# Three small reorderings on the matrix engine of a two-layer hybrid decoder: chunk states signalled one by one, value products half a gate later, spare products in other gaps

## What is computed

```
mod = silu(c) @ w_ada[l] + b_ada[l]                   # conditioning: six vectors of 1024
h   = rms_norm(x) * (1 + sc1) + sh1
gq, gk, gv, ga, gr, sq, sk, sv, mix_a, mix_b = split(h @ w_in[l])
# gated linear attention, 4 heads, chunks of 64 tokens (8 chunks):
o_intra = (causal(q_dec @ k_inv^T)) @ v
S[n+1]  = decay[n] * S[n] + k_end[n]^T @ v[n]         # a scan over the chunks
o       = o_intra + q_dec[n] @ S[n]                   # then rms_norm and a gate
# sliding attention, 8 heads, windows of 128, softmax with sinks:
p = softmax(q @ k_band^T);  o_swa = p @ v_band
x = x + g1 * ((sigmoid(mix_a) * (o @ w_up_gla) + sigmoid(mix_b) * (o_swa @ w_up_swa)) @ w_out)
x = x + g2 * moe(rms_norm(x) * (1 + sc2) + sh2)       # 16 experts, top 2
```

## Time and profile before

| | |
|---|---|
| median of three runs | 1501.91 us |
| profiled execution | 1501.6 us, span 1499.9 us |
| mean granted clock of PE | 0.969 |
| PE busy | 1383.6 us, 92% of the span |
| DVE busy | 982.4 us, 65% |
| ACT busy | 726.9 us, 48% |
| chain that ended last | PE 77%, DVE 7%, DMA 6%, ACT 3% |

### The profile page before, as it was taken

One profiled execution on the slowest core, in us unless ns is written; L12 is line 12 of the kernel. 1 busy time (PEld: TensorE's weight loads), 2 busy tenths in 40 slices (PEclk: granted clock), 3 DMA queues, 4 the chain that ended last, 5 costly groups with the idle time before them and its releaser, 6 DMA issues.

```text
span 1499.9 us, 18822 instructions
## 1 busy us (share of the span) xinstructions
PE 1383.6 (92%) x7109; PEld 1093.3 (73%) x7110; DVE 982.4 (65%) x934; ACT 726.9 (48%) x776; POOL 294.9 (20%) x255
## 2 busy tenths in 40 slices
PE   3999999999999899999949999999998899999893
PEld 1776877666677788888738787788787788888572
DVE  4334575324477899999971567632657889999294
ACT  4324355122155677777652536513325677777260
POOL 1000000000015244545220000000003334544130
PEclk9999999999999999999979999999998999999997
DMA  9766302776684899999842230131355899999365
GB/s 299 270 225 233 132 1 85 259 246 218 218 330 145 301 365 393 386 378 380 316 133 85 85 113 1 57 112 57 140 213 194 296 347 366 374 377 386 147 248 192
DMA packets 157267, 341.37 MB, mean 228 GB/s; under 512 B 17150, under 2 KB 19394, under 8 KB 157186
## 3 DMA queue, kind: packets, MB, share of 16 engines
q1 hardware_dynamic: 141170, 316.97, 58.4%
q0 software_dynamic: 16016, 23.30, 4.6%
HBM read 350.68 MB, written 23.61 MB: 250 GB/s over the span
## 4 chain that ended last, share of the span: by engine, by line
PE 77%; DVE 7%; DMA 6%; ACT 3%; issue 3%; DVEq 2%; SPq 1%; POOL 0%; POOLq 0%; ACTq 0%
PE PS L1180 15%; PE PS L1181 14%; PE PS L1182 14%; PE PS L1576 7%; PE PS L1580 7%; PE PS L1584 7%; PE PS L1114 3%; PE PS L1564 2%; DMA ring<-in_w_ada 2%; DMA ring<-in_w_down 1%; ACT reg L934 1%; DVE ring_parts L2190 1%; DMA y_rows<-reg,icur 1%; PE PS L1589 1%; SPq L475 1%
## 5 line engine op out<-in xcount | busy, mean ns | idle before, releaser
L1180 PE MATMUL PS<-ring_parts 128*128 128x512 f32 (+1 forms) x704 | 276.7, 393 | 9.5 <-DVE hT_parts L1820 5.9
L2190 DVE TENSOR_TENSOR ring_parts<-ring,reg_parts 128x2048 fp32r<-128x2048 f32 x124 | 278.1, 2284 | 3.4 <-ACT reg_parts L1038 3.4
L1038 ACT ACTIVATE reg_parts<-ring 128x2048 fp32r<-128x2048 f32 x124 | 230.6, 1909 | 67.4 <-DMA ring<-in_w_down 35.3
L1812 DVE TENSOR_TENSOR ring_parts<-ring,ring_parts 128x2048 fp32r<-128x2048 f32 (+1 forms) x52 | 112.9, 2210 | 153.9 <-ACT ring_parts L856 153.9
L1180 PEld LDWEIGHTS PS<-ring_parts 128*128 128x128 f32 x704 | 133.3, 189 | 63.9 <-issue 31.0
L856 ACT ACTIVATE ring_parts<-ring 128x2048 fp32r<-128x2048 f32 (+1 forms) x52 | 93.4, 1845 | 151.9 <-DMA ring<-in_w_in 113.4
L2190 DVE TENSOR_TENSOR ring_parts<-ring,hT_parts 128x2048 fp32r<-128x2048 f32 x68 | 155.2, 2287 | 13.5 <-issue 13.0
L1182 PE MATMUL PS<-ring_parts 128*128 128x512 f32 x384 | 150.5, 392 | 0.0
L1181 PE MATMUL PS<-hT_parts,ring_parts 128*128 128x512 f32 x384 | 150.5, 392 | 0.0
L1038 ACT ACTIVATE hT_parts<-ring 128x2048 fp32r<-128x2048 f32 x68 | 126.5, 1909 | 14.0 <-DMA ring<-in_w_gate 8.0
L1584 PE MATMUL PS<-ring_parts,reg_parts 128*128 128x512 f32 x528 | 130.6, 389 | 0.0
(11 more groups left out here) (328 smaller groups left out, 2406.2 us busy)
## 6 DMA issues: line engine op xcount, KB each, us to landing
ring<-in_w_up SPq DMA_DIRECT2D x32, 2048.0 KB
ring<-in_w_gate SPq DMA_DIRECT2D x32, 2048.0 KB, 12.5
ring<-in_w_down SPq DMA_DIRECT2D x32, 2048.0 KB
ring<-in_w_ada SPq DMA_DIRECT2D x40, 1024.0 KB, 5.3
ring<-in_w_in SPq DMA_DIRECT2D x16, 2048.0 KB
ring<-in_w_ada SPq DMA_DIRECT2D x4, 2048.0 KB, 12.4
ring<-in_w_out SPq DMA_DIRECT2D x4, 2048.0 KB
reg<-y_rows SPq DMA_DIRECT2D x16, 512.0 KB, 6.3
```

The source lines that it names most:

```text
L1038: act.activation(high[:, cols], ring[:, 3 * k + part, cols], ACT.Copy).then_inc(w_hi[part], 1)
L1180: pe.matmul(out_, left[0], right[0], start=first, stop=False)
L1812: tt(ring_r[:, unit_slot(n), cols], w, ring_r[:, 2 + n % 2, cols].bitcast(F32), ALU.subtract).then_inc(lo_done, 1)
L2190: tt(ring_r[:, 3 * k + part, cols], ring[:, 3 * k + part, cols], high[:, cols].bitcast(F32), ALU.subtract).then_inc(w_lo[part], 1)
```

## The change

Three edits of order and signalling; the arithmetic that the output depends on is the same.

- The seven states are signalled one by one: each pair of L1921 increments the semaphore, and PE waits, ahead of each of the seven chunks of the first half `m = 0`, for that chunk's state only.
- `values(0)` comes one gate half later: after `early_gate(1, 1)` instead of ahead of it.
- In layer 0 the eight spare products ahead of the key/value projection go, with their wait for `ht_full`; ten stand between `condition_columns` and `first_unit(2)`. In layer 1 six are added between the transposes and the key/value projection, behind that wait.

```diff
-        s_done = counted("states_ready", 1)
+        s_done = counted("chunk_states_ready", NCH - 1)
...
                     condition_columns(FIRST_BANKS[0], 1)
+                    spare_products(10, FIRST_BANKS[1])
                     first_unit(2)
                     pe.wait_ge(ada_added, 1)
                     transpose_tokens(range(6, 7))
-                    pe.wait_ge(ht_full, at(ht_full, l, 1))
-                    spare_products(8, 0)
                 else:
...
                                 mm.then_inc(ht_ready, 1)
+                    pe.wait_ge(ht_full, at(ht_full, l, 1))
+                    spare_products(6, 0)
...
-                pe.wait_ge(s_done, at(s_done, l, 1))
                 for m in range(2):
                     for n in range(1, NCH):
+                        if m == 0:
+                            pe.wait_ge(s_done, at(s_done, l, n))
...
                 early_gate(1, 0)
+                early_gate(1, 1)
                 values(0)
-                early_gate(1, 1)
                 transpose_probs(1, 0)
...
                 for m in range(2):
-                    dve.tensor_copy(S[:, m, 1, :], PS[:, 4 + 2 * m, 0:P])
+                    step = dve.tensor_copy(S[:, m, 1, :], PS[:, 4 + 2 * m, 0:P])
+                step.then_inc(s_done, 1)
...
-                step.then_inc(s_done, 1)
+                    step.then_inc(s_done, 1)
```

## The result

The changed kernel takes 1492.11 us in the median of 20 runs (1487.47 to 1495.65), the kernel before 1500.99 in 20 runs beside them (1494.38 to 1505.09). The ratio is 0.9941, with a 95% interval from 0.9929 to 0.9952: 8.9 us less, against 9.4 forecast on the medians. The profiled execution of the changed kernel is the fastest of its 20, 1487.5 us with a span of 1485.8. So the two traces lie 14.1 us apart, 5 us more than the medians; that much is the spread between executions, and I take gains from stretches, not from the ends.

A forecast was written before the change was run, and what follows sets the result against it. PE, busy for 92% of the span, was taken as the bound, through its waits and half clock. Terms of 1.7 + 2.5 + 1.4 + 1.5 + 2.0 = 9.1 us off 1501.6 gave 1492.5 us, range 1489.5 to 1499.5.

The forecast's parts named there:

- Opening of layer 0: Layer 0's start: eight spare products leave PE's path, ten added in a wait cost nothing; 1.7 us gained.
- the limit: Layer 0's opening: the fourth unit's DMA, there at about 40.4 us, becomes the new limit, with no wait.
- States: State products: the 1.24 us wait goes and full clock holds behind them; 2.5 us in layer 0, 2.0 in layer 1.
- The six extra waits: State products: six more, already fulfilled waits were taken to cost 0.4 us against the gain.
- The first rival: States and layer 1's opening: clock falls even without the wait; 4.7 us gained, 1496.9 us; all lost-clock cases together 0.33.
- The drained array: States: each of seven waits stops PE loading weights ahead, 0.5 us each; 1503.0 us in all; chance 0.04.
- First values: Sliding attention: second window's transposes start 1.9 us earlier in layer 0, 1.4 us left; 0 in layer 1.
- The new wait: Ahead of second window's transposes, 1.7 us; its rival: it lowers the clock in both layers, 1494.8 us, within lost-clock 0.33.
- Opening of layer 1: Layer 1's key/value projection: six spare products hold the clock, sixteen passes take 0.13 instead of 0.227 us; 1.5 us gained.
- Downstream: Behind the edits: gains travel to the end; rival, swallowed if experts' weights come no earlier, 1500 to 1502 us, chance 0.13.

The follow-up runs named there:

- e3: Kernel before with only layer 0's spare products moved (eight gone, ten added in the earlier wait); 1501.54 against 1501.33 us, ratio 1.0000.
- e6: Changed kernel without the ten spare products in layer 0's opening; 1492.90 us against 1501.52 for the kernel before, ratio 0.9937.
- e7: Changed kernel with twenty spare products instead of ten in layer 0's opening; 1493.64 us against 1499.67 for the kernel before, ratio 0.9950.
- e8: Changed kernel with a wait ahead of each of the 28 state products instead of 7 waits; 1491.02 us against 1499.67 for the kernel before, ratio 0.9944.
- e11: Changed kernel with ACT's root table load ahead of the late weight unit's high parts; 1490.16 us against 1501.52 for the kernel before, ratio 0.9913.
- e1: Kernel before with only the seven states signalled one by one; 1494.97 against 1501.33 us, ratio 0.9956.
- e4: Kernel before with only the six spare products in layer 1's opening added; 1497.10 against 1501.33 us, ratio 0.9968.
- e12: Kernel before with only layer 1's six spare products added, run a second time; 1497.77 against 1501.52 us, ratio 0.9961.
- e10: Changed kernel without the six spare products of layer 1's opening; 1492.19 us against 1499.67 for the kernel before, ratio 0.9946.
- e2: Kernel before with only values(0) moved half a gate later; 1499.85 against 1501.33 us, ratio 0.9995.
- e5: Kernel before with the last head's four products inside the chunks made twice, ahead of the states' wait; 1497.46 against 1499.67 us, ratio 0.9977.

## Why the prediction was right, point by point

**Opening of layer 0 (1.7 forecast).** Over the traces the start of the products inside the chunks lies at 174.46 us on average with the edit (172.85 to 176.26) and at 175.91 without (174.33 to 178.42): 1.45, no more than the traces of one kind differ among themselves. The pair of before and after has 1.06, and e3, with this edit alone, shows no shorter time. So this term is the least sure of the five. That the ten cost nothing and earn nothing was right (e6, e7), and so was the limit. But the fourth unit lands at about 41.0 us (40.70 to 41.08 in the five traces in which PE waits for it), not at 40.4. The sum also counted no give-back at the wait of 2.15 us.

**States (2.5 and 2.0).** The mechanism was right; three sizes were not. The six extra waits cost 0.05 us a layer where 0.4 was taken off. The tail of the state products ran at half clock too (4.25 against 3.40 us), and I didn't count that. So the pair of traces shows 3.6 and 2.4 us. Against this, the fall came in six of ten sections only, so that the mean over the traces is 14.85 to 12.1 in layer 0, 2.75 us, and 14.95 to 13.5 in layer 1, 1.45 (of the kernels signalled one by one the six in which ACT's late table load is the bound). The sum took the trace of before as what always happens. Together the two layers come to 4.2 us against 4.5 forecast, and that is in part luck: what was counted too low and what was counted as certain nearly cancel. The first rival, that the clock falls all the same, is out: the clock held in all eighteen sections without the gap. The rule of the Trainium skill, TensorE: Matmul & The Clock Gate, in the table of "Why this matters for your kernels", on which that rival leaned, warns only of longer gaps. These traces do not agree with it: half clock followed the gap of 1.24 us in six of ten sections, and in none of the eighteen where it was removed or mostly filled. The drained array is out as well (e8). Layer 1 gains less because ACT is late there, as predicted; e11 shows by what, and so does e1, where the weight unit came 1.2 us earlier in the section, which took 12.17 us.

**First values (1.4 and 0).** 1.45 and 0.00, in every trace with the edit against every one without. The transposes follow DVE at once, and 0.45 of the 1.9 us is taken back at the low parts of the weights, where PE still waits 0.62 us. Without the edit half clock followed the wait of 2.00 us in layer 0 in all six traces. The new wait lowered no clock; that rival is out.

**Opening of layer 1 (1.5).** 1.5 in the pair and 1.5 to 2.5 over the traces, eight with the six against six without. The products end later than the forecast had them: of the wait of 2.90 us 0.40 is left behind them. What stays open is why e4 and e12 gain 4 us in the median while leaving the six out costs nothing in e10. The half clock at the router of layer 1, longer in e1, e2, e3, e5 and before than in e4, e12 and e10, would go with both, but what sets it no run here shows.

**Downstream.** The gain went through to the end; the longer wait for a conditioning half in the pair is within what that wait varies by. The sum of the means is 1.45 + 2.75 + 1.45 + 1.5 + 1.45 = 8.6 us, against 8.9 measured (7.2 to 10.7 by the interval) and 9.4 forecast. The interval alone would not tell this from a sum with one term missing; the sections do. In the medians the single edits come to 6.4 + 1.5 - 0.2 + 4.2 = 11.9; those without the six to 7.7, and e10, which has just these, gives 7.5. Of the 14.1 us between the two profiled executions 3.8 lie behind the second layer's sliding attention, in stretches without an edit: that is spread between executions, or what the router of layer 1 adds.

## What to carry to other kernels

A short wait of the matrix engine is worth more than its length if half clock follows it; signal what it waits for in pieces, since a wait that is already fulfilled cost next to nothing here (28 as little as seven). Count such a fall by how often it comes over several traces, not by the one at hand. And before covering a wait for a transfer, look at the next transfer: twenty spare products won 1.5 us of clock, and the next unit's landing took them back.

## What was not expected

The same wait of 1.24 us with the same instructions around it was followed by a granted clock of 0.5 six times in ten. The wait of 2.00 us ahead of the first values was so six times in six in layer 0; in layer 1 of the same six traces it lasts 1.62 to 1.64 us, and half clock followed it never. The one of 2.15 us near 52 us was so seven times in fourteen, and the two of 1.8 us never in the changed kernel. A longer wait alone is therefore no sure sign. The runs of either kernel spread over 8 to 11 us.

Moving one table load on ACT ahead of a copy that waits for a transfer was worth 1.25 us of the section, about as much as the states' signalling won in that layer.
